# Mixture-of-experts loop: in the iterations of small expert blocks, GpSimd issues the fetch of rows ahead of the mask for the output sum

## What is computed

```python
def swiglu(x, w1, w3, w2):
    return (jax.nn.silu(x @ w1) * (x @ w3)) @ w2

def expert_block(args):
    e, toks, gs = args
    xb = t[toks]
    return swiglu(xb, w1[e], w3[e], w2[e]) * gs[:, None]

out = lax.map(expert_block, (block_e, row_tok..., row_g...))
routed = jax.ops.segment_sum(out.reshape(rows, D), row_tok, num_segments=n_tok)
shared = swiglu(t, ws1, ws3, ws2)
```

## Time and profile before

| | us |
|---|---|
| median of 3 runs | 1027.86 (1023.93 to 1028.11) |
| profiled execution | 1019.35 |
| its span, first to last instruction | 1017.5 |
| expert loop, POOL's first and last L938 | 657.7 to 1006.5 |
| PE, DVE, ACT, POOL busy in the span | 95%, 74%, 57%, 41% |
| TensorE's granted clock | 0.994 of full speed |

### The profile page before, as it was taken

The page is one execution under the profiler, slowest core; times in us unless marked ns, Lnnn a source line. Parts: engine busy times, 40 slices in busy tenths (PEclk is TensorE's granted clock), DMA queues, the critical chain, the costliest instruction groups (busy, mean ns, idle before and its releaser), DMA issues. The chain is left out here.

```text
span 1017.5 us, 16364 instructions
## 1 busy us (share of the span) xinstructions
PE 968.3 (95%) x5072; PEld 775.5 (76%) x5072; DVE 750.4 (74%) x1322; ACT 580.1 (57%) x896; POOL 418.1 (41%) x373
## 2 busy tenths in 40 slices
PE   7999999999999899999979998899999999999996
PEld 6778877778766676778768888678787787778874
DVE  4678888768854454457686755498898988898988
ACT  4555655455433533243535532588887888888875
POOL 5164453223300000023223321466777767777675
PEclk9999999999999999999989999999999999999998
DMA  9877676776844416336233321988888888888883
GB/s 309 290 255 260 223 259 231 259 241 196 288 159 146 139 51 239 106 113 198 105 132 117 126 83 51 364 336 314 346 315 340 345 312 344 320 326 343 325 325 146
DMA packets 79430, 238.58 MB, mean 234 GB/s; under 512 B 12876, under 2 KB 19077, under 8 KB 66066
## 3 DMA queue, kind: packets, MB, share of 16 engines
q1 hardware_dynamic: 66146, 196.60, 53.0%
q0 software_dynamic: 12656, 40.91, 11.6%
q10 hardware_dynamic: 576, 0.41, 0.1%
HBM read 235.58 MB, written 2.16 MB: 234 GB/s over the span
## 5 line engine op out<-in xcount | busy, mean ns | idle before, releaser
L1919 PE MATMUL bank<-w_hi,a_hi 128*128 128x512 f32 (+2 forms) x512 | 205.9, 402 | 10.7 <-DVE w_lo L1333 9.0
L1919 PE MATMUL bank<-w_hi,a_lo 128*128 128x512 f32 (+2 forms) x512 | 197.2, 385 | 0.0
L1919 PE MATMUL bank<-w_lo,a_hi 128*128 128x512 f32 (+2 forms) x512 | 196.9, 385 | 0.0
L1333 DVE TENSOR_TENSOR w_lo<-ring,w_hi 128x1024 fp32r<-128x1024 f32 (+2 forms) x134 | 155.5, 1182 | 49.6 <-ACT w_hi L1016 44.8
L1016 ACT ACTIVATE w_hi<-ring 128x1024 fp32r<-128x1024 f32 (+2 forms) x140 | 141.3, 1024 | 78.3 <-PE bank L1919 74.6
L1732 DVE TENSOR_TENSOR up_lo<-raw_weights,up_hi 128x1024 fp32r<-128x1024 f32 x120 | 146.3, 1255 | 0.0
L1181 ACT ACTIVATE up_hi<-raw_weights 128x1024 fp32r<-128x1024 f32 x136 | 135.9, 1054 | 0.0
L1919 PEld LDWEIGHTS bank<-w_hi,a_hi 128*128 128x128 f32 x512 | 96.8, 189 | 39.1 <-issue 20.6
L809 POOL TENSOR_SCALAR mean_squares<-mean_squares 128x8 f32<-128x8 f32 (+2 forms) x32 | 9.9, 310 | 279.9 <-ACT logits L969 199.2
L1919 PEld LDWEIGHTS bank<-w_hi,a_lo 128*128 128x128 f32 x512 | 96.6, 189 | 19.9
L1919 PEld LDWEIGHTS bank<-w_lo,a_hi 128*128 128x128 f32 x512 | 97.0, 189 | 18.5 <-issue 1.4
(11 more groups left out here) (284 smaller groups left out, 1904.1 us busy)
## 6 DMA issues: line engine op xcount, KB each, us to landing
raw_weights<-in_w_dram SPq DMA_DIRECT2D x102, 1024.0 KB, 7.0
ring<-in_w_in_dram SPq DMA_DIRECT2D x58, 1024.0 KB, 6.0
merged<-in_w_ada_dram POOLq DMA_DIRECT2D x96, 256.0 KB, 4.2
ring<-in_w_out_dram SPq DMA_DIRECT2D x8, 1024.0 KB, 5.8
ring<-in_w_branch_dram SPq DMA_DIRECT2D x6, 1024.0 KB, 4.8
bias<-rel_rows SPq DMA_DIRECT2D x40, 128.0 KB, 4.9
ring<-in_ws_dram SPq DMA_DIRECT2D x2, 1024.0 KB, 4.9
merged<-in_x_dram SPq DMA_DIRECT2D x2, 512.0 KB, 5.2
```

The source lines that it names most:

```text
L1333: dve.tensor_tensor(w_parts[1][:, 2 * p:2 * p + 2, 0:w], view(JOB[it[1:3]], kind)[:, 2 * p:2 * p + 2, :], w_parts[0][:, 2 * p:2 * p + 2, 0 ...
L1919: mm = pe.matmul(ps[:, 0:wide], a_parts[za][:, k, t * P:(t + 1) * P], w_parts[zw][:, k, 0:wide], start=start, stop=stop)
```

## The change

In the odd iterations the mask moves behind the gather, so that even and odd iterations have the same order. Nothing is added or removed.

```diff
                         make_pick(i + 3, (r + 3) % BODY, m4 + 1 + (r + 3) // BODY)
-                        if r % 2:
-                            make_put(i, r)
                         gather_rows(i + 2, (r + 2) % BODY, m4 * (BODY // 2) + (r + 2) // 2)
-                        if not r % 2:
-                            make_put(i, r)
+                        make_put(i, r)
```

## The result

| | before | changed |
|---|---|---|
| median of 9 runs | 1023.88 us (1021.71 to 1028.11) | 1017.52 us (1015.09 to 1019.41) |
| profiled execution | 1019.35 us | 1015.71 us |
| its span | 1017.5 us | 1013.9 us |

Measured again later, the same pair of kernels gave 0.9951 (0.9933 to 0.9969), with medians 4.3 us apart. The direction is right and the size is off by a factor of about two. The first three runs of the kernel before had a median of 1027.86; with nine runs it is 1023.88, so that 4.0 us of the error of 7.9 us lie in the level that the gain was subtracted from, and 3.9 us in the gain.

A forecast was written before the change was run, and what follows sets the result against it. PE was taken to bound the kernel. Only the small gather's wait counted, -2.5 us, other terms zero: 1027.86 - 2.5 = 1025.4 us. The range ran from 1019.9 to 1028.11 us, with 1 us more for a small loss.

The forecast's parts named there:

- What bounds the kernel, and the place of the gain: Expert loop: PE works nearly all the time; gaps varying between pairs total 4.0 us, 2.5 before the small transposes.
- the wait at L2162: PE's wait before the transposes of the small block's rows, caused by the late small gather: goes in all pairs, -2.5 us.
- the wait at L2169: PE's wait before the transposes of large rows: 1.5 us in three pairs, change in time taken as zero.
- The step from the profiled execution to the median: The median of the runs shown lay 8.5 us above the profiled execution; this difference was carried over unchanged.
- The gather's start and landing: Small gather on POOL: starts 3.1 us earlier, 4.2 us behind L931; lands 4.4 to 6.6 us later, the longer taken.
- The length of the issue: Small gather's issue on POOL, at its new place ahead of the mask: 1.2 to 1.6 us.
- the issue of the large gather: On POOL behind the two picks: moves by -2.6 to +0.1 us, counted as zero time, with 1.1 us of room.
- Mask and scatter: The mask, moved back on POOL, ends by 783.0, 3.7 us before the scatter at L2177 reads it: zero cost.
- The slower rival: DVE's `up_lo` run holds back the small gather and POOL's work slides: +8 us, about 1036 us; chance 0.07.
- The 0.6 us beyond the landing of 6.6 us: Delay of the small gather from which the slower case was to decide; alternatively 1.1 us at the large gather.
- More than the forecast: Picks start earlier, the large gather goes out 1 to 2.6 us sooner, L2169's waits go too: -4.0 us, 1023.9; chance 0.12.

The follow-up runs named there:

- second execution: The kernel before, unedited, timed again against itself: ratio 1.0003; its profiled execution took 1030.44 us.
- first execution: The profiled execution of the kernel before that the prediction read, no edit: 1019.35 us.
- four executions: All profiled executions of the kernel before, no edit: 1019.35, 1030.44, 1022.66 and 1024.92 us.

## Why the prediction was wrong, point by point

- **What bounds the kernel, and the place of the gain**: right. In the execution that the prediction read, PE's gaps at the two gathers were nearly all that varied in the loop, and they are gone; the loop's mean pair is 317.8 / 15 = 21.19 us, where the shortest pair before was 21.16.
- **The term that was mis-sized is the wait at L2162.** I took it from one execution, as 2.5 us. In four it is 2.4, 3.3, 4.9 and 6.3, 4.2 in the mean. The reasoning stopped at the usual pair, in which landing and use touch. When a landing and its use touch, every delay of a transfer goes straight to PE, and the delays vary between executions: landings of 5.5 to 6.0 us in place of 4.4 in three pairs of the second execution. The first execution had none above 4.7. That its time lay below all three runs shown was the warning.
- **The second term is the wait at L2169, which the sum put at zero.** It is 0.2 to 2.2 us in the four executions, 1.4 in the mean, and none is left in the changed kernel.
- **The step from the profiled execution to the median failed.** The difference of 8.5 us was carried over "unchanged", as if it had nothing to do with the gathers. 4.0 us of it were the three runs themselves, whose median was that much above that of nine. The other 4.5 us agree roughly with the four executions, which are longer than the first in the mean by 2.5 us in the loop, at these very waits, and by 2.5 us ahead of it. The part ahead of the loop was rightly carried over; the part in the loop belonged to the gain. The range was cut too narrow for both.
- **The gather's start and landing**: 4.1 us behind L931 as forecast; the landing is 5.6 us after issue, within the bounds 4.4 and 6.6 and nearer to the one taken (over the loop 5.4 to 6.8 us). A full queue lengthened it, as was said: of the 275 GB/s between 781 and 782 in the stretches below, the small rows are 254 and the weights 21, so the rows moved when the weights had ended. The issue is 3.1 us earlier behind L931 and the landing, 4.1 + 5.6 = 9.7 us behind it instead of 7.3 + 4.4 = 11.7, 2.0 us; that is room enough for the late landings.

```profile
780.00:781.00 1.00, 1.00 (x6) 0.82 (x5) 1.00 (x1) 1.00 (x2) 1.00 (x1) 1.00 0.93 393
781.00:782.00 1.00, 1.00 (x6) 0.80 (x5) 0.83 (x3) 1.00 (x3) 1.00 (x2) 1.00 0.98 275
782.00:783.00 1.00, 1.00 (x6) 0.79 (x5) 1.00 (x5) 1.00 (x2) 0.92 (x2) 1.00 0.04 8
783.00:784.00 1.00, 1.00 (x6) 0.82 (x5) 1.00 (x2) 1.00 (x2) 0.31 (x1) 1.00 0.77 123
```

- **The length of the issue**: 1.97 us, above the 1.2 to 1.6 forecast, and the mask 2.12, below the 2.93. Together with the picks (1.19 for 3.36) POOL is busy 377.7 us instead of 418.1. For the issue of the large gather I had allowed -2.6 to +0.1 us, and it came 2.0 us earlier.
- **Mask and scatter**: the mask is done at 781.75 and nobody waits for it, as forecast.
- **The slower rival** did not happen. The gather's issue did get longer beside DVE, by 0.7 us, but it had 1.8 us of room. (The 0.6 us beyond the landing of 6.6 us, from which it was to decide, do not follow from its rows: from 785.0 to the present landing at 785.9 are 0.9 us.) What can be lost in this way is shown by the picks: 0.53 us of shift against DVE's `down_lo` costs 2.0 us of their length, and in the kernel with all gathers first PE waits for them. The rule of the Trainium skill, page "SBUF — State Buffer", section "SBUF: two separate sides", that the second of the two operations blocks, agrees with the trace in its direction there: the picks that start just ahead of `down_lo` take 3.21 us for 1.19.
- **"More than the forecast", the large gather profits too**: its result, -4.0 us, is nearly that of the profiled executions (-3.6). Its mechanism, the earlier issue, is one of two ways to that gain. With the large gather alone early those waits are gone; but with its issue held at 12.1 or 13.3 us and the small gather early they are down to 0.2 or 0.3 us as well. The second way I had not seen: the small rows no longer share the DMA engines with the next up weights, the weights end sooner, and the large rows behind them with these.

## What to carry to other kernels

Where a landing and its use touch in the usual case, one profiled execution can give the lower end of what the wait costs, as it did here; read several, and give such a transfer the microsecond or two by which its landing varies. An instruction of GpSimd may take nearly three times as long when it starts half a microsecond later beside VectorE (3.21 us for 1.19), so a change of order is read from the lengths at the new place and from who waits for the instruction that moved back. And do not push a fetch ahead of everything: here the next step forward, past the picks, lost 23 us against the step before (1043.06 against 1019.77).

## What the runs showed of the hardware that I had not expected

The two picks, 128x128 each, take 1.19 us when they end as VectorE's run of two-input subtractions begins and 3.21 us when they start 0.5 us ahead of it. VectorE's own run of three `up_lo` took 3.50 us beside the gather's issue and the mask, 3.69 us beside the mask and the first half microsecond of the issue. A large gather issued 12.1 or 13.3 us behind L931 landed at 19.8 in both cases: within that range its transfer is set by the traffic, not by its issue. And a wait of PE can cost more than its length: behind waits of 1.64 and 1.47 us the granted clock was at its lower level for 3.4 us.
